# Row-wise weight products on one Trainium2 core: the high and low weight matmuls of each left block, in two passes or in pairs

## The chip, the cores and the metric

One core of a Trainium2 chip runs the whole program in one launch. The metric is the device time of one execution in microseconds (us); the times shown are of three executions of the kernel before.

## The reference, cut to what matters

The program computes two transformer blocks of two layers each on 256 tokens of width 2048, all in float32. Most of its arithmetic is products of the token rows with weights: input projections, output projections and an MLP.

```python
x = first_block(x, ...)                  # 2 layers: h @ w_in, three mixers, y @ w_out
for l in range(DEPTH):                   # 2 layers of the second block
    h = rms_norm_2(x, attn_norm[l])
    proj = h @ w_in[l]
    ...                                  # three attention mixers
    x = x + mixed @ w_o[l]
    h = rms_norm_2(x, mlp_norm[l])
    x = x + jnp.square(jax.nn.relu(h @ w_up[l])) @ w_down[l]
```

## The kernel before, in words

**The products.** TensorE multiplies rounded float32 numbers (fp32r), so each operand is split into a high part (the rounded value) and a low part (what the rounding left). A product is high x high, high x low and low x high, all added up in PSUM. The left operand (the rows, transposed, in `hT_both`, `cT_hi`/`cT_lo` or `uT_hi`/`uT_lo`) is the 128x128 block that stands still in the array; the weights stream past it, 344 to 512 columns in one matmul.

**The weight groups.** The weights come in 988 groups of up to 128 x 1024 numbers, numbered L in the one order in which all products use them. For each group SP issues a load into one of 10 slots of `raw` (line 790); ScalarE copies it, rounded, into one of 4 slots of `w_hi` (line 874, semaphore `hi_ready`); VectorE subtracts that from the raw numbers and leaves the low part in the same bytes, now called `w_lo` (line 1251, semaphore `group_read`); TensorE multiplies by both, and the last matmul counts `group_multiplied`, which frees the slot of `w_hi` and the slot of `raw`. ScalarE and VectorE convert groups two ahead of the one that TensorE is at (`AHEAD = 2`). VectorE also multiplies 192 loads of modulation weights, which use the same slots of `raw` (lines 1407 and 1419), and does much of the mixers' work.

**A row-wise group.** `group_product` (lines 1987 to 2013) does this for all jobs except the up-projections (`high_turned` and `low_turned`, lines 2024 and 2034, where the weights stand still) and two small head-wise products (`heads_product`). A group of 1024 numbers at 512 columns has two chunks c, and there are two token halves t, so four terms (c, t), each with its own left block; the two halves t go to two PSUM banks. Before the change TensorE runs three passes over the four terms: line 2005 multiplies by the high weights, then it waits for `group_read`, line 2008 multiplies the same four left blocks by the low weights, and line 2012 multiplies the low left blocks by the high weights. Where the left operand is still being made (the first groups of a job), the first pass waits for its high part and the last for its low part. The last groups of three jobs are done for one token half at a time (`tail`), so that the first half is ready sooner; there all terms of a pass go to one PSUM bank.

**The order around it.** Each engine has its instructions written in its own fixed order. On TensorE, before the product of group L stand the transposes that prepare left operands (line 1951), and at places listed in tables (`SLIDING_AT`, `LINEAR_AT`, `MLA_AT` and others) the steps of the attention mixers: scores (line 2207), probabilities times values (line 2228), and so on. A matmul that waits therefore holds up every later one, the mixers' too. `busy` (line 2083 before, 2082 after) multiplies the identity by itself a few times while TensorE would idle.

Of the kernel before, what the change touches and what calls it, by code (L numbers as in the profile page):

```python
# [212 lines left out]
def build(nc, io):  # L213
    ctx = ExitStack()
    with ctx:
# [51 lines left out]
        def blocks(ring, slot, cnt, width):  # L267

            return ring[:, slot, 0:cnt * width].rearrange("p (c n) -> p c n", n=width)
        w_hi = sb("w_hi", [P, SPLIT_SLOTS, GROUP], F32R)  # L270

        def hi_blocks(slot, cnt, width):

            pitch = (width + 3) // 4 * 4
            return blocks(w_hi, slot, cnt, pitch)[:, :, 0:width]
# [159 lines left out]
        group_at = []  # L435
# [165 lines left out]
        def pinned(job, i):  # L601

            return job.pinned and i == job.turns

        def bank(job, i, t):

            if job.swept and i == 2 or pinned(job, i):
                return 4 + t
            return 2 * ((job.T + i) % 2) + t
# [1317 lines left out]
        def _(pe):  # L1927
# [26 lines left out]
            def multiply(job, i, j, L, led_to):  # L1954
# [23 lines left out]
                if not job.in_tail(i, j):  # L1978
                    group_product(job, i, j, L, range(TOK), led_to).then_inc(S.group_multiplied, 1)
                    return  # L1980
                mm = group_product(job, i, j, L, (0,), led_to)
                if j == len(job.groups) - 1:
                    mm.then_inc(S.first_token, 1)
                    for back in reversed(range(job.tail)):
                        group_product(job, i, j - back, L - back, (1,)).then_inc(S.group_multiplied, 1)

            def group_product(job, i, j, L, tokens, led_to=None):

                hi, lo = job.lhs
                k0, cnt = job.groups[j]  # L1990
                start, stop = k0 == 0, k0 + cnt == job.chunks
                if pinned(job, i):
                    start, stop = start and job.kind == "ina", stop and job.kind == "ind"
                terms = [(c, t, ps[:, bank(job, i, t), 0:job.width]) for c in range(cnt) for t in tokens]
                wh = hi_blocks(L % SPLIT_SLOTS, cnt, job.width)
                wl = blocks(w_lo, group_at[L] % RAW_SLOTS, cnt, job.width)

                def rows(v, c, t):

                    return v[:, job.lhs0 + k0 + c, t * P:(t + 1) * P]  # L2000
                pe.wait_ge(S.hi_ready, L + 1)
                if led_to:
                    pe.wait_ge(S.lhs_hi, led_to[0])
                for c, t, o in terms:
                    pe.matmul(o, rows(hi, c, t), wh[:, c], start=start and c == 0, stop=False)  # L2005
                pe.wait_ge(S.group_read, group_at[L] + 1)
                for c, t, o in terms:
                    pe.matmul(o, rows(hi, c, t), wl[:, c], start=False, stop=False)  # L2008
                if led_to:
                    pe.wait_ge(S.lhs_ready, led_to[1])  # L2010
                for c, t, o in terms:
                    mm = pe.matmul(o, rows(lo, c, t), wh[:, c], start=False, stop=stop and c == cnt - 1)  # L2012
                return mm
# [377 lines left out]
```

## Time and profile before

| | |
|---|---|
| median of 3 executions | 2918.69 us (2916.41 to 2918.80) |
| span of the profiled execution, first to last instruction | 2916.5 us |
| the profiled execution's own time | not listed apart; its span lies 2.2 us below the median |
| TensorE matmul busy | 2835.1 us, 97% of the span, 14688 matmuls |
| TensorE weight load busy | 2448.1 us, 84%, 14688 loads |
| VectorE busy | 1892.8 us, 65% |
| ScalarE busy | 1442.6 us, 49% |
| mean granted TensorE clock | 0.995 of full |

A matmul's busy time includes its way through the array, so two that follow each other closely overlap in the trace. What a stream of them costs is the distance from one start to the next. A row of the time line with x4 merges four, from the first start to the last end.

### The profile page before, as it was taken

Reading aid. Unit: us, or ns where it says so; the run is one execution under the profiler, and the core shown is the slowest. Engines: PE = TensorE matmul, PEld = TensorE weight load, DVE = VectorE, ACT = ScalarE, POOL = GpSimd, SP = SyncE. Lnnn points to the kernel's source line nnn. Section 1 sums busy time; section 2 is a strip of 40 time slices with the busy share of each in tenths; the row PEclk is TensorE's granted clock in tenths of the full one; section 3 lists DMA queues with packets and bytes.
Section 4 is the critical chain, followed back from the end, with each engine's and each line's share of the span. In section 5 each row is a group of like instructions: output and inputs, shape, how many; then the busy total and the mean of one; then the engine's idle time right before and its main releaser. Section 6 shows DMA issues by size and latency. Waiting matters only on the chain.

```text
span 2916.5 us, 37048 instructions
## 1 busy us (share of the span) xinstructions
PE 2835.1 (97%) x14688; PEld 2448.1 (84%) x14688; DVE 1892.8 (65%) x2395; ACT 1442.6 (49%) x2035; POOL 41.1 (1%) x48
## 2 busy tenths in 40 slices
PE   5998998999999999999999999999999999999998
PEld 5886787898889988888888888899888888888887
DVE  8998998779755566665445554545666654456554
ACT  5445544665546554644334444555546443344443
POOL 0000000000000000000000000000000000000000
PEclk9999999999999999999999999999999999999999
DMA  9996598767655455555665556564445555555653
GB/s 392 366 350 227 188 363 305 257 203 256 241 177 181 146 162 165 176 191 191 194 195 188 188 194 193 176 189 152 160 164 174 190 195 192 194 187 191 207 195 137
DMA packets 173884, 611.89 MB, mean 210 GB/s; under 512 B 19681, under 2 KB 19953, under 8 KB 173073
## 3 DMA queue, kind: packets, MB, share of 16 engines
q1 hardware_dynamic: 170912, 600.42, 60.4%
q0 software_dynamic: 1824, 6.61, 0.8%
q8 instruction: 117, 1.92, 0.3%
q10 hardware_dynamic: 976, 2.51, 0.3%
q14 instruction: 55, 0.44, 0.0%
HBM read 607.34 MB, written 2.11 MB: 209 GB/s over the span
## 4 chain that ended last, share of the span: by engine, by line
PE 86%; DVE 7%; ACT 3%; DMA 2%; issue 1%; SPq 0%; POOL 0%; POOLq 0%; ACTq 0%; DVEq 0%
PE ps L2005 19%; PE ps L2008 19%; PE ps L2012 18%; PE ps L2024 16%; PE ps L2034 8%; PE ps L1951 2%; DVE w_lo L1251 2%; DVE raw L1407 2%; PE ps L2228 1%; DMA raw<-in_w_ina 1%; PE ps L2207 1%; ACT w_hi L874 1%; DMA raw<-in_w_modT 1%; DVE proj L1381 1%; DMA raw<-in_w_in 0%
## 5 line engine op out<-in xcount | busy, mean ns | idle before, releaser
L1251 DVE TENSOR_TENSOR w_lo<-raw,w_hi 128x1024 fp32r<-128x1024 f32 (+4 forms) x988 | 1150.0, 1175 | 865.6 <-ACT w_hi L874 863.0
L874 ACT ACTIVATE w_hi<-raw 128x1024 fp32r<-128x1024 f32 (+4 forms) x988 | 994.6, 1018 | 1174.6 <-PE ps L2012 644.4
L2005 PE MATMUL ps<-w_hi,hT_both 128*128 128x512 f32 (+3 forms) x1824 | 479.3, 384 | 16.4 <-DVE proj L1381 8.4
L2024 PE MATMUL ps<-hT_both,w_hi 128*128 128x512 f32 x2048 | 490.2, 391 | 0.9 <-DVE u L1355 0.9
L2008 PE MATMUL ps<-w_lo,hT_both 128*128 128x512 f32 (+3 forms) x1824 | 463.0, 375 | 0.6 <-DVE w_lo L1251 0.6
L2012 PE MATMUL ps<-w_hi,hT_both 128*128 128x512 f32 (+3 forms) x1824 | 460.1, 374 | 0.0
L2024 PEld LDWEIGHTS ps<-hT_both,w_hi 128*128 128x128 f32 x2048 | 376.1, 188 | 74.1 <-DVE u L1355 1.3
L2008 PEld LDWEIGHTS ps<-w_lo,hT_both 128*128 128x128 f32 x1824 | 340.2, 189 | 51.0 <-DVE w_lo L1251 1.9
L2012 PEld LDWEIGHTS ps<-w_hi,hT_both 128*128 128x128 f32 x1824 | 339.7, 189 | 48.7
L2005 PEld LDWEIGHTS ps<-w_hi,hT_both 128*128 128x128 f32 x1824 | 327.0, 189 | 63.7 <-DVE proj L1381 12.5
L2005 PE MATMUL ps<-w_hi,uT_hi 128*128 128x512 f32 x1024 | 275.1, 390 | 0.0
L2008 PE MATMUL ps<-w_lo,uT_hi 128*128 128x512 f32 x1024 | 274.4, 389 | 0.0
L2012 PE MATMUL ps<-w_hi,uT_lo 128*128 128x512 f32 x1024 | 274.4, 389 | 0.0
L2034 PEld LDWEIGHTS ps<-hT_both,w_lo 128*128 128x128 f32 x2048 | 262.8, 191 | 10.2
L2034 PE MATMUL ps<-hT_both,w_lo 128*128 128x256 f32 x2048 | 265.9, 283 | 0.0
L2008 PEld LDWEIGHTS ps<-w_lo,uT_hi 128*128 128x128 f32 x1024 | 192.2, 188 | 40.1
L2012 PEld LDWEIGHTS ps<-w_hi,uT_lo 128*128 128x128 f32 x1024 | 192.2, 188 | 40.0
L2005 PEld LDWEIGHTS ps<-w_hi,uT_hi 128*128 128x128 f32 x1024 | 191.5, 188 | 39.3
L1407 DVE SCALAR_TENSOR_TENSOR raw<-raw,c_row 128x1024 f32<-128x1024 f32 x176 | 212.7, 1219 | 0.8
L1496 DVE TENSOR_TENSOR hT_both<-hf,hT_both 128x512 fp32r<-128x512 f32 x80 | 55.3, 691 | 54.1 <-ACT hT_both L943 53.5
L1110 ACT ACTIVATE probs<-probs,smax 128x128 f32<-128x128 f32 (+3 forms) x112 | 50.9, 455 | 40.3 <-DVE smax L1576 38.0
L1951 PE MATMUL ps<-cst,proj 128*128 128x128 f32 x292 | 42.2, 276 | 25.2 <-ACT proj L1194 23.8
(255 smaller groups left out, 1563.7 us busy)
## 6 DMA issues: line engine op xcount, KB each, us to landing
raw<-in_w_up SPq DMA_DIRECT2D x256, 512.0 KB, 4.1
raw<-in_w_down SPq DMA_DIRECT2D x256, 512.0 KB, 4.2
raw<-in_w_modT SPq DMA_DIRECT2D x192, 512.0 KB, 5.6
raw<-in_w_rest SPq DMA_DIRECT2D x80, 456.0 KB, 3.4
raw<-in_w_z SPq DMA_DIRECT2D x64, 512.0 KB, 4.4
raw<-in_w_out SPq DMA_DIRECT2D x64, 512.0 KB, 4.4
raw<-in_w_rest SPq DMA_DIRECT2D x48, 344.0 KB, 3.6
raw<-in_w_oa SPq DMA_DIRECT2D x32, 512.0 KB, 3.4
```

The source lines that it names most:

```text
L874: act.activation(hi_blocks(L % SPLIT_SLOTS, c, w), blocks(raw, G % RAW_SLOTS, c, w), ACT.Copy).then_inc(S.hi_ready, 1)
L1110: a = act.activation(e, e, ACT.Exp, bias=smax[:, r, j:j + 1], accum_out=ssum[:, r, j:j + 1])
L1251: dve.tensor_tensor(blocks(w_lo, r, c, w), blocks(raw, r, c, w), hi_blocks(s, c, w).bitcast(F32), ALU.subtract).then_inc(S.group_read, 1)
L1381: dve.tensor_tensor(v, v, ps[:, b:b + TOK, 0:job.width], ALU.add).then_inc(S.dve_evacuated, 1)
L1407: dve.scalar_tensor_tensor(out=w, in0=w, scalar=1.0, in1=c_row[:, part], op0=ALU.mult, op1=ALU.mult, accum_out=mod_part[:, l, block, part: ...
L1496: dve.tensor_tensor(dst_lo[:, 2 * b:2 * b + 2], hf[:, u_ % 2], dst_hi[:, 2 * b:2 * b + 2].bitcast(F32), ALU.subtract).then_inc(S.lhs_ready, 1)
L1951: mm = pe.transpose(ps[0:rows, b, j * P:(j + 1) * P], s, ident)
L2005: pe.matmul(o, rows(hi, c, t), wh[:, c], start=start and c == 0, stop=False)
L2008: pe.matmul(o, rows(hi, c, t), wl[:, c], start=False, stop=False)
L2012: mm = pe.matmul(o, rows(lo, c, t), wh[:, c], start=False, stop=stop and c == cnt - 1)
L2024: pe.matmul(ps[:, bank(job, i, f)], wh[:, c, f * P:(f + 1) * P], hT_both[:, k0 + c].rearrange("p a n -> p (a n)"), start=k0 + c == 0, stop ...
L2034: mm = pe.matmul(ps[:, bank(job, i, f), 0:2 * P], wl[:, c, f * P:(f + 1) * P], hT_hi[:, k0 + c], start=False, stop=k0 + c == job.chunks - 1)
```

## The change

In `group_product` the first two passes become one: for each term (c, t) the matmul by the high weights is followed directly by the matmul of the same left block by the low weights, into the same PSUM bank. The wait for `group_read`, which stood ahead of the second pass, now stands ahead of the first matmul of the group. The third pass stays. Every matmul is still issued, with the same operands. The diff:

```diff
                 pe.wait_ge(S.hi_ready, L + 1)
+                pe.wait_ge(S.group_read, group_at[L] + 1)
                 if led_to:
                     pe.wait_ge(S.lhs_hi, led_to[0])
                 for c, t, o in terms:
                     pe.matmul(o, rows(hi, c, t), wh[:, c], start=start and c == 0, stop=False)
-                pe.wait_ge(S.group_read, group_at[L] + 1)
-                for c, t, o in terms:
                     pe.matmul(o, rows(hi, c, t), wl[:, c], start=False, stop=False)
                 if led_to:
                     pe.wait_ge(S.lhs_ready, led_to[1])
```

TensorE's order at a group of the down-projection in the second block (`uT_hi`, `uT_lo` are the left operand), before:

```order
L2005 MATMUL ps<-w_hi,uT_hi 128x512 [waits hi_ready,u_split]
L2005 MATMUL ps<-w_hi,uT_hi 128x512 x3
L2008 MATMUL ps<-w_lo,uT_hi 128x512 [waits group_read]
L2008 MATMUL ps<-w_lo,uT_hi 128x512 x3
L2012 MATMUL ps<-w_hi,uT_lo 128x512 x4
```

and of the changed kernel, whose lines 2006, 2007 and 2011 are the high, the low and the last product:

```order
L2006 MATMUL ps<-w_hi,uT_hi 128x512 [waits group_read,hi_ready,u_split]
L2007 MATMUL ps<-w_lo,uT_hi 128x512
L2006 MATMUL ps<-w_hi,uT_hi 128x512
L2007 MATMUL ps<-w_lo,uT_hi 128x512
L2006 MATMUL ps<-w_hi,uT_hi 128x512
L2007 MATMUL ps<-w_lo,uT_hi 128x512
L2006 MATMUL ps<-w_hi,uT_hi 128x512
L2007 MATMUL ps<-w_lo,uT_hi 128x512
L2011 MATMUL ps<-w_hi,uT_lo 128x512 x4
```

The two passes of four have become four pairs, and the wait for `group_read` has moved up by four matmuls. The same on TensorE in the last input projection of the first block (`rest`, 344 columns), where the scores of the sliding-window mixer (line 2207, 2206 after) stand behind a group; before:

```order
L2005 MATMUL ps<-w_hi,hT_both 128x344 [waits hi_ready]
L2005 MATMUL ps<-w_hi,hT_both 128x344 x3
L2008 MATMUL ps<-w_lo,hT_both 128x344 [waits group_read]
L2008 MATMUL ps<-w_lo,hT_both 128x344 x3
L2012 MATMUL ps<-w_hi,hT_both 128x344 x4
L2207 MATMUL ps<-k1T,q1T 128x256 [waits dve_bank_drained]
L2207 MATMUL ps<-k1T,q1T 128x256 x3
```

and after:

```order
L2006 MATMUL ps<-w_hi,hT_both 128x344 [waits group_read,hi_ready]
L2007 MATMUL ps<-w_lo,hT_both 128x344
L2006 MATMUL ps<-w_hi,hT_both 128x344
L2007 MATMUL ps<-w_lo,hT_both 128x344
L2006 MATMUL ps<-w_hi,hT_both 128x344
L2007 MATMUL ps<-w_lo,hT_both 128x344
L2006 MATMUL ps<-w_hi,hT_both 128x344
L2007 MATMUL ps<-w_lo,hT_both 128x344
L2011 MATMUL ps<-w_hi,hT_both 128x344 x4
L2206 MATMUL ps<-k1T,q1T 128x256 [waits dve_bank_drained]
L2206 MATMUL ps<-k1T,q1T 128x256 x3
```

The mixer's scores stand where they stood, behind the group's last product. The orders of VectorE, ScalarE, GpSimd and of the DMA queue do not move.

## Rows read from the trace of the kernel before

**Rows 1.** The page, part 1: busy time, share of the span, instructions
```profile
PE 2835.1 (97%) x14688; PEld 2448.1 (84%) x14688; DVE 1892.8 (65%) x2395; ACT 1442.6 (49%) x2035; POOL 41.1 (1%) x48
```
**Rows 2.** Windows: stretch, length, busy us of PE, PEld, DVE, ACT, POOL, clock, DMA, GB/s
```profile
100.00:150.00 50.00, 46.38 (x227) 41.32 (x226) 49.90 (x72) 21.21 (x25) 0.00 (x0) 1.00 0.97 367
...
600.00:700.00 100.00, 99.41 (x608) 91.33 (x607) 82.71 (x143) 59.47 (x95) 1.28 (x1) 1.00 0.70 235
```
**Rows 3.** Groups by line: busy us, mean ns of one, then idle before them, releaser
```profile
L1251 DVE TENSOR_TENSOR w_lo<-raw,w_hi 128x1024 fp32r<-128x1024 f32 x734 | 891.2, 1224 | 708.2 <-ACT w_hi L874 706.8
L874 ACT ACTIVATE w_hi<-raw 128x1024 fp32r<-128x1024 f32 x734 | 768.6, 1057 | 981.7 <-PE ps L2012 540.0 <-PE ps L2034 366.0 <-DMA raw<-in_w_out 37.2
```
**Rows 4.** The page, part 5: the second pass of `group_product` from `hT_both`
```profile
L2008 PE MATMUL ps<-w_lo,hT_both 128*128 128x512 f32 (+3 forms) x1824 | 463.0, 375 | 0.6 <-DVE w_lo L1251 0.6
```
**Rows 5.** Time line, down-projection, first and second tile: start, length (us), engine, line
```profile
1366.52 1.07 PE L2012 MATMUL ps<-w_hi,uT_lo 128*128 128x512 f32 x4
1367.43 1.07 PE L2005 MATMUL ps<-w_hi,uT_hi 128*128 128x512 f32 x4
...
1440.87 1.07 PE L2005 MATMUL ps<-w_hi,uT_hi 128*128 128x512 f32 x4
...
1441.77 1.07 PE L2008 MATMUL ps<-w_lo,uT_hi 128*128 128x512 f32 x4
1442.22 1.23 DVE L1251 TENSOR_TENSOR w_lo<-raw,w_hi 128x1024 fp32r<-128x1024 f32 x1 [1.49 <-ACT w_hi L874]
```
**Rows 6.** Chain of waits, an up-projection (256 columns) and a product of the linear mixer
```profile
359.02 2.69 PE ps L2301 x24
...
1195.34 1.91 PE ps L2034 x16
```
**Rows 7.** Time line: transposes (all blocks different), identity by itself (one block repeated)
```profile
469.04 1.04 PE L1951 MATMUL ps<-cst,proj 128*128 128x128 f32 x8
...
858.26 2.40 PE L2083 MATMUL ps<-cst 128*128 128x128 f32 x20
```
**Rows 8.** One line asked for, L2083: count, duration min/median/max
```profile
L2083 PEld LDWEIGHTS ps<-cst x84: 188/192/338, 31.7 to 862.8; 128*128 128x128 f32 x84
L2083 PE MATMUL ps<-cst x84: 273/275/582, 31.7 to 862.9; 128*128 128x128 f32 x84
```
**Rows 9.** Time line near the end, one token half, all in one PSUM bank
```profile
2898.94 0.62 PE L2005 MATMUL ps<-w_hi,uT_hi 128*128 128x512 f32 x2
2899.39 0.61 PE L2008 MATMUL ps<-w_lo,uT_hi 128*128 128x512 f32 x2
2899.84 0.62 PE L2012 MATMUL ps<-w_hi,uT_lo 128*128 128x512 f32 x2
```
**Rows 10.** Time line of the second group of the program (450 columns)
```profile
39.19 2.10 DVE L1251 TENSOR_TENSOR w_lo<-raw,w_hi 128x900 fp32r<-128x900 f32 x2 [0.15 <-ACT w_hi L874]
...
39.38 0.98 PE L2005 MATMUL ps<-w_hi,hT_both 128*128 128x450 f32 x4
...
40.34 0.70 PEld L2008 LDWEIGHTS ps<-w_lo,hT_both 128*128 128x128 f32 x4 [0.35 <-DVE w_lo L1251]
```
**Rows 11.** Time line in the 344-column projection
```profile
575.00 2.45 DVE L1251 TENSOR_TENSOR w_lo<-raw,w_hi 128x688 fp32r<-128x688 f32 x3 [2.25 <-ACT w_hi L874]
...
575.02 0.90 PE L2005 MATMUL ps<-w_hi,hT_both 128*128 128x344 f32 x4 [0.69 <-ACT w_hi L874]
...
575.93 0.89 PE L2008 MATMUL ps<-w_lo,hT_both 128*128 128x344 f32 x4
...
654.37 2.44 DVE L1251 TENSOR_TENSOR w_lo<-raw,w_hi 128x688 fp32r<-128x688 f32 x3
...
655.30 0.89 PE L2008 MATMUL ps<-w_lo,hT_both 128*128 128x344 f32 x4 [0.59 <-DVE w_lo L1251]
```
**Rows 12.** Time line around a fall of the clock (450 columns)
```profile
197.90 1.46 PE L2005 MATMUL ps<-w_hi,hT_both 128*128 128x450 f32 x4 [2.50 <-DVE proj L1381]
...
202.01 0.98 PE L2005 MATMUL ps<-w_hi,hT_both 128*128 128x450 f32 x4
```

## The prediction, made before the changed kernel ran

> **What bounds the kernel now.** I read the page first: TensorE is busy 97% of the span, VectorE 65%, ScalarE 49% [rows 1]. Matmuls overlap in that account, so next the stretches: from 600 us on TensorE fills over 99 us of nearly every 100 (the first such stretch is shown), while in the first 200 us the DMA engines are filled to 0.97 or more and TensorE has 46 of 50 us [rows 2]. So a load bound holds at the start, TensorE itself for the last 2300 us. Then the groups by line, to see how far the conversions run ahead: the subtraction (line 1251) idles for ScalarE's copy, and the copy idles for TensorE to free a slot [rows 3]. Both wait for their customer, so they are early. The second pass, the one whose wait the change moves, waited 0.6 us for line 1251 in the whole run [rows 4]. Last the time line, for the distance from one matmul to the next.
>
> **The price of one matmul.** In the down-projection two passes of four 512-column matmuls start 0.90 or 0.91 us apart [rows 5], and in the tail two start 0.45 us apart [rows 9]: 0.226 us each, about 0.2267 where more of them are averaged. At 2.4 GHz, which the granted clock of 1.00 is [rows 2], 512 columns take 213.3 ns; 13.4 ns are left over. 16 matmuls of 256 columns take 1.91 us [rows 6], so 119.4 each: 106.7 of columns and 12.7 over. The distance follows the columns. The weight load of each, of which there are as many as matmuls [rows 1], lies beside the matmul ahead of it. Only with 128 columns does it show: transposes start (1.04-0.275)/7 = 0.109 us apart [rows 7, 8], where the columns are 53 ns.
>
> **Part 1, the order of the matmuls.** Nothing is removed or added: 2868 pairs of the lines 2005 and 2008 (1824 from `hT_both`, 1024 from `uT_hi`, 20 from `cT_hi`) and their weight loads are all issued, in another order. Three things differ for a matmul.
>
> (a) The second of a pair has the left block of the first. Whether the repeated load costs less isn't in the trace for these shapes. From below: if no load were needed and everything above the columns went with it, 13.4 ns would be saved in each second matmul, 2868 x 0.0134 = 38 us. From above: the identity multiplied by itself, the same block again and again, starts (2.40-0.275)/19 = 0.112 us apart, against 0.109 of transposes with a new block each [rows 7]; 3 ns more in each would be 2868 x 0.003 = 9 us lost. Those 84 matmuls have 84 loads of the full 188 ns [rows 8]: repetition saves no load. And ordinary mixer products with changing blocks also take 2.69/24 = 0.112 [rows 6], so the 3 ns belong to the form and not to the repetition. I take 0 for (a), by rows 7 and 8, the only ones with a repeated block.
>
> The Trainium skill ("TensorE: Matmul & The Clock Gate", Back-to-back issue gap) gives N / 2.4 + 2.5 ns for matmuls that follow each other, 215.8 ns at 512 columns. The trace's 226.7 doesn't agree. If the 10.9 ns between them were the new weights' and fell away in every second matmul of a pair, the rule would give an estimate of 31 us saved; by the rows it is none.
>
> (b) Both matmuls of a pair add into one PSUM bank, at the same addresses; before, the two token halves took turns. The tail of the last job already does this: with one token half all matmuls of its passes, and across the passes, go to one bank, and they start 0.226 us apart as everywhere else [rows 5, 9]. 0.
>
> (c) The stream changes between `w_hi` and `w_lo` at each matmul. Across the change of pass it did so before, and 1440.87 to 1441.77 holds such a change at no extra [rows 5]. 0.
>
> **Part 2, the wait that moves up.** `group_read` must now be there before the first matmul, four matmuls earlier (0.91 us at 512 columns, 0.81 at 450, 0.62 at 344). I paired the k-th subtraction of line 1251 with the first matmul of the k-th group, for the 720 groups of `group_product`. In the down-projections the subtraction ends 5.6 us before its group begins in the typical case: one that starts at 1442.22 and takes 1.23 [rows 5] is for the group that TensorE reaches at about 1449.0, two groups of 12 x 0.2267 = 2.72 us after 1443.6. There the wait is always met. In 12 groups it isn't.
> - Second group of the program: the first of the two subtractions ends at 40.28, its low pass began at 40.34 [rows 10]. Now the first pass begins there, and the end moves by that pass, 0.81 us. The groups at 71.86 (subtraction over at 72.86), 116.07 (116.73) and 159.32 (159.97), read from the time line in the same way, give 0.81, 0.63 and 0.62; four small ones (36.8 to 66.6 us) 0.06 + 0.16 + 0.08 + 0.03. Together 3.2 us before 160 us.
> - The 344-column groups at 575.02 and 653.92: their low passes began 0.06 us after the subtraction ended, at 575.93 and 655.30 [rows 11]. Each moves by 0.62.
> - Three more at 694.65, 1038.61 and 2061.51, where the first pass began about 0.1 us before the subtraction's end: 0.19 + 0.15 + 0.15. Together 1.7 us after 570 us.
>
> The first 3.2 us fall in the stretch that loads bound: TensorE has about 3.6 us of slack in every 50 there [rows 2], a group late by 0.8 us makes it up before 200 us, and the loads it releases have others in flight before them. I cost them at 0; if that cover is gone, they cost their 3.2. The last 1.7 us fall where TensorE has no slack, so they reach the end. What is queued behind the waiting matmul is the group's other eleven and then, at 575 us, the scores of the sliding-window mixer, which come 0.62 us later; VectorE, which waits for scores, had idled 2.25 us before its subtractions there [rows 11] and can take that. The release of the slot is at the group's end as before, and moves by no more.
>
> **Part 3, several waits on one matmul.** The first matmul of a group now carries two or three waits (`hi_ready`, `group_read`, `u_split`). In the down-projection's first tile it had two before, and there the last pass of one group (1366.52) and the first of the next (1367.43) are 0.91 us apart, no more than within a group [rows 5]. I take 0; three on one matmul I can bound only by that, 0 again.
>
> Sum: 2916.5 + 0 + 1.7 = 2918.2 for the profiled execution's span; its own time isn't listed, the median of the three is 2.2 us above the span, so 2918.7 + 1.7 = 2920.4 us for the median. That is 0.06%; a difference under about 0.2% (5.8 us) can't be told from none for this kernel, whose three executions spread over 2.4 us.
>
> **The rivals.**
> 1. *The repeated left block makes the second matmul cheaper.* For it: a distance 13 ns above the columns' time in every matmul, so there is something to win, and loads busy 84% of the span [rows 1]. Against: the identity's loads are all there and start no closer [rows 7, 8]; the distance follows the columns, so the load isn't what TensorE waits for [rows 5, 6]. Price: up to 38 us, 2920.4 - 38 = 2882; at half, 2901. It decides from 2.6 ns a pair on, (5.8+1.7)/2868. Chance 0.09. A small saving of ScalarE's or VectorE's by other timing adds 0.01 on this side.
> 2. *The early wait spreads, slower.* Place: the first 200 us and the mixers of the second layer, 570 to 700 us. The 3.2 us of the start are not absorbed, since each late release delays a load in the stretch where loads bound, and TensorE's longer pauses let its clock fall. At 197.90, after 2.50 us of idling, three passes took until 202.01, 4.11 us for 12 matmuls that take 12 x 0.2035 = 2.44 at full clock [rows 12]: 1.7 us a fall. Two more falls and the 3.2: 2920.4 + 3.2 + 3.4 = 2927.0. It decides when more than 5.8 us of waits reach the end. Against: all direct delays together are 4.9 us, and the pauses at 575 and 654 us, 0.69 and 0.59 us now [rows 11], come to 0.69 + 0.91 = 1.6 and 655.30 - 654.07 = 1.2 us (the pass before ends at 654.07), less than the 2.50 after which the clock fell. Chance 0.11. The skill's same page (A second HAM failure mode) says that short pauses between groups of matmuls can make the clock swing; by that this rival would come true, and the pause at 575 us in this trace, with the clock at full, doesn't show it.
> 3. *Pairs in one bank or with one block cost some ns.* The upper bound of (a), 9 us: 2929. Against: rows 9. Chance 0.03.
>
> **How the numbers follow.** Forecast 0.76, rivals 0.10, 0.11, 0.03. The forecast's own range is 2916.4 (the fastest of before) to 2918.7 + 4.9 = 2923.6. With 0.24 outside it, one rival has to be taken in, and the slower one lies nearer: to 2928. At the low end I allow 1 ns a pair, 3 us, from 2918.7 + 0 down: 2915. Faster by over 0.2%: 0.10; within: 0.76; slower: 0.14.
>
> **What the profile would show.** Right: the merged rows of the lines 2006 and 2007 alternate, 0.227 us apart; 14688 loads and matmuls as now; line 2006 waits for line 1251 at about 40, 72, 116, 159, 575 and 654 us, 3 to 5 us in all; the group of eight still takes 8 x 0.227 = 1.81 us. Wrong in (a): starts at 0.213 to 0.22 us at every second matmul, or fewer loads than 14688. Wrong in (b): starts alternating 0.227 and more. Wrong in part 2: a sum of waits of line 2006 on line 1251 above 6 us, or more falls of the clock than the first 500 us have now.

## The result and the profile after

Five executions each, in the same rounds: before 2916.41 us in the median, after 2925.58 us (2924.67 to 2929.75), a ratio of 1.0030 with a 95% interval of 1.0019 to 1.0042. That is 9.2 us slower, inside the range of the prediction, but beyond its forecast of 1.7 us. A second comparison of 11 executions with 33 of before (below, `after_again`) gave 1.0019 (1.0010 to 1.0028), 6.1 us. The two medians put the loss at 0.2 to 0.3%; the intervals reach from 0.1 to 0.4%.

The 33 executions of before in the second comparison spread over 9.5 us (2913.2 to 2922.7), and most of that goes with the time that TensorE's clock was at its lower level. The mean clock of each execution is recorded to three places: the 12 at 0.994 had a mean span of 2917.6 us, the 12 at 0.995 one of 2915.7, the 8 at 0.996 one of 2912.7. So a single trace can't show a loss of a few us by its span; places have to be compared. The profiled execution of after (2929.75 us, span 2927.8) was the slowest of its five.

The page of after, part 1 and two groups of part 5:

```profile
PE 2840.2 (97%) x14688; PEld 2451.9 (84%) x14688; DVE 1893.7 (65%) x2395; ACT 1442.4 (49%) x2035; POOL 41.0 (1%) x48
...
L1251 DVE TENSOR_TENSOR w_lo<-raw,w_hi 128x1024 fp32r<-128x1024 f32 (+4 forms) x988 | 1149.9, 1175 | 871.9 <-ACT w_hi L874 868.6
...
L2007 PE MATMUL ps<-w_lo,hT_both 128*128 128x512 f32 (+3 forms) x1824 | 685.3, 376 | 0.0
```

All 14688 weight loads are still there, no fewer than in [rows 1]. The mean length of the low-weight matmul is 376 ns, 375 in [rows 4]. Its group's busy time has gone from 463 to 685 us without any more work: the four of a pass used to overlap each other, and now each overlaps its neighbours of the other line.

The distance from one matmul to the next, in the time line of after in a down-projection, and in the tail, where everything goes to one bank:

```profile
1452.20 0.39 PE L2006 MATMUL ps<-w_hi,uT_hi 128*128 128x512 f32 x1
1452.42 0.39 PE L2007 MATMUL ps<-w_lo,uT_hi 128*128 128x512 f32 x1
1452.65 0.39 PE L2006 MATMUL ps<-w_hi,uT_hi 128*128 128x512 f32 x1
1452.88 0.39 PE L2007 MATMUL ps<-w_lo,uT_hi 128*128 128x512 f32 x1
...
1453.56 1.07 PE L2011 MATMUL ps<-w_hi,uT_lo 128*128 128x512 f32 x4
1454.46 0.39 PE L2006 MATMUL ps<-w_hi,uT_hi 128*128 128x512 f32 x1
...
2910.51 0.39 PE L2007 MATMUL ps<-w_lo,uT_hi 128*128 128x512 f32 x1
2910.74 0.39 PE L2006 MATMUL ps<-w_hi,uT_hi 128*128 128x512 f32 x1
```

High to low, 0.22 to 0.23 us; low to high, 0.23; a pass of four 0.90; across a group's start, which now carries three waits, no more. It is what [rows 5, 9] show of before. From the group at 1149.35 us of before to the one at 1814.84, 665.49 us, after takes 665.49 us too.

Who waited for the subtraction, in the answer on line 1251 of after:

```profile
  ACT w_hi L874: 868.6, 629
who waited for it (us, times):
  PE ps L2006: 5.5, 8
```

8 waits, 5.5 us, against 0.6 us in [rows 4]. Two of them, at the 344-column projection:

```profile
583.88 2.45 DVE L1251 TENSOR_TENSOR w_lo<-raw,w_hi 128x688 fp32r<-128x688 f32 x3 [2.25 <-ACT w_hi L874]
...
584.90 0.39 PE L2006 MATMUL ps<-w_hi,hT_both 128*128 128x344 f32 x1 [1.71 <-DVE w_lo L1251]
...
663.99 2.44 DVE L1251 TENSOR_TENSOR w_lo<-raw,w_hi 128x688 fp32r<-128x688 f32 x3
...
665.00 0.40 PE L2006 MATMUL ps<-w_hi,hT_both 128*128 128x344 f32 x1 [1.32 <-DVE w_lo L1251]
```

They are the groups of [rows 11]: the subtraction starts as late as before, relative to its surroundings, and TensorE stands 1.71 and 1.32 us where it stood 0.69 and 0.59. A ninth wait, 0.79 us at the second group, is put down to ScalarE's copy (below); with it the sum is 6.3 us, just over the 6 us that the prediction had named as a sign against part 2. Aligned by group, the trace of after is 2.5 us late at 200 us, 8.9 at the start of the 344-column projection, 10.6 after it, and 10.9 from there to 2000 us.

In the stretch between, the start of the second layer, the clock of this trace fell twice more than in before. The windows, and the pause ahead of the second fall:

```profile
500.00:510.00 10.00, 7.76 (x27) 5.89 (x27) 9.36 (x13) 4.61 (x6) 0.00 (x0) 0.83 0.83 326
520.00:530.00 10.00, 6.80 (x28) 5.18 (x28) 7.01 (x10) 3.73 (x6) 0.00 (x0) 0.90 0.99 350
```

```profile
527.52 0.47 PE L2006 MATMUL ps<-w_hi,hT_both 128*128 128x512 f32 x1 [3.20 <-ACT hT_both L943]
...
529.02 0.63 PE L2006 MATMUL ps<-w_hi,hT_both 128*128 128x512 f32 x1
529.44 0.63 PE L2007 MATMUL ps<-w_lo,hT_both 128*128 128x512 f32 x1
```

After 3.20 us of idling the matmuls come to be 0.42 to 0.43 us apart, which is 512 columns at 1.2 GHz. More falls than before were another sign that the prediction had named. Whether these falls belong to the change was the first thing to find out.

### The profile page after: what moved, and what is told of

The parts are those of the page before. It is cut to its first block, busy times and chain, and to the rows that moved or that the text cites. A ratio compares the mean times of both kernels' runs of the same rounds, so it can differ in the third digit from the quotient of the medians.

```text
span 2927.8 us, 37578 instructions
## 1 busy us (share of the span) xinstructions
PE 2840.2 (97%) x14688; PEld 2451.9 (84%) x14688; DVE 1893.7 (65%) x2395; ACT 1442.4 (49%) x2035; POOL 41.0 (1%) x48
## 4 chain that ended last, share of the span: by engine, by line
PE 86%; DVE 6%; DMA 3%; ACT 3%; issue 1%; SPq 0%; POOL 0%; POOLq 0%; ACTq 0%; DVEq 0%
PE ps L2006 19%; PE ps L2007 19%; PE ps L2011 18%; PE ps L2023 16%; PE ps L2033 8%; PE ps L1951 2%; DVE w_lo L1251 2%; DVE raw L1407 2%; PE ps L2227 1%; DMA raw<-in_w_ina 1%; PE ps L2206 1%; ACT w_hi L874 1%; DMA raw<-in_w_modT 1%; DMA raw<-in_w_in 1%; DVE proj L1381 0%
## 5 line engine op out<-in xcount | busy, mean ns | idle before, releaser
L2006 PE MATMUL ps<-w_hi,hT_both 128*128 128x512 f32 (+3 forms) x1824 | 702.3, 385 | 21.5 <-ACT hT_both L943 7.6
L2007 PE MATMUL ps<-w_lo,hT_both 128*128 128x512 f32 (+3 forms) x1824 | 685.3, 376 | 0.0
L2011 PE MATMUL ps<-w_hi,hT_both 128*128 128x512 f32 (+3 forms) x1824 | 459.0, 373 | 0.0
L2006 PEld LDWEIGHTS ps<-w_hi,hT_both 128*128 128x128 f32 x1824 | 346.1, 190 | 76.5 <-issue 12.0
L2006 PE MATMUL ps<-w_hi,uT_hi 128*128 128x512 f32 x1024 | 399.0, 390 | 0.0
L2007 PE MATMUL ps<-w_lo,uT_hi 128*128 128x512 f32 x1024 | 398.5, 389 | 0.0
L2007 PEld LDWEIGHTS ps<-w_lo,hT_both 128*128 128x128 f32 x1824 | 346.5, 190 | 44.2
L2011 PEld LDWEIGHTS ps<-w_hi,hT_both 128*128 128x128 f32 x1824 | 339.3, 188 | 48.7
```

## The experiments

Theory A: the moved wait is the whole loss, and the pairs are free. Theory B: a pair costs some ns. In the tables of a result "before" is the kernel before in the same rounds on the same chip.

### The wait alone, and the pairs by place

`wait_up` keeps the three passes and moves the wait:

```diff
                 if led_to:
                     pe.wait_ge(S.lhs_hi, led_to[0])
+                pe.wait_ge(S.group_read, group_at[L] + 1)
...
-                pe.wait_ge(S.group_read, group_at[L] + 1)
```

> The three passes as before, only the wait for group_read stands ahead of the first pass. Theory A (the moved wait is all of the loss, the pairs cost nothing): as slow as the change, about +9 us (+6 to +12), with more falls of the clock than before between 200 and 540 us. Theory B (the pairing itself costs, 9 us over 2868 pairs, 3 ns each): within 3 us of before.

`pairs_second` and `pairs_first` choose by group between the body of the change and that of before:

```diff
+                if L >= jobs["c20"].L:
+                    pe.wait_ge(S.group_read, group_at[L] + 1)
+                    for c, t, o in terms:
+                        pe.matmul(o, rows(hi, c, t), wh[:, c], start=start and c == 0, stop=False)
+                        pe.matmul(o, rows(hi, c, t), wl[:, c], start=False, stop=False)
+                else:
...
```

> Pairs and the early wait in the second block only (from c20 on, 863 us into the trace of before), passes in the first. Theory A: +0.3 us (two waits of 0.15), not to be told from before. Theory B: 3 ns for each of the pairs there, about 2150 of 2868, +6.5 us.

> Pairs and the early wait in the first block only. Theory A: all of the loss, about +9 us, all of it before 700 us. Theory B: about 700 of the 2868 pairs, +2 us.

> The change once more, on the chip and in the rounds of the other three: +7 to +12 us against before. The number of falls of the clock in its profile tells whether the two more (at 504 and 528 us) belong to every execution; theory A says the waits come again at the same places, and the falls may not.

| kernel | median us, 11 executions | ratio to before (2917.88 us, 33) | 95% interval |
|---|---|---|---|
| wait_up | 2922.40 | 1.0014 | 1.0005 to 1.0023 |
| pairs_second | 2917.49 | 1.0003 | 0.9995 to 1.0012 |
| pairs_first | 2924.10 | 1.0021 | 1.0012 to 1.0029 |
| after_again | 2924.02 | 1.0019 | 1.0010 to 1.0028 |

The counts of pairs in these expectations were off: 1056 lie in the first block and 1812 in the second, so theory B wanted 3.2 and 5.4 us. It falls all the same: the 1812 cost at most 3.5 us by the interval, and the wait alone, without a pair, costs 4.5 us. The 665.49 us above say the same. But 4.5 us is under the 6 to 12 us expected of `wait_up`, and the 6.1 us of `after_again` under its 7 to 12: A is right on where the loss comes from, and these expectations, taken from the first comparison, were too large.

The falls of the clock are not the mechanism. Before the last 10 us, the traces of before, `pairs_second` and `pairs_first` hold 27 us at the lower clock each, `after_again` 31, and `wait_up`, slower than before in the median, 17. In the mean over the executions the clock is 0.99455 for `after_again` and 0.99482 for before, a difference worth about 0.8 us of the 6. At the same recorded clock of 0.994 the mean spans are 2923.1 us (8 executions) and 2917.6 us (12). The two falls at 504 and 528 us made this one trace long.

### Where the first block loses

`pairs_start` has the pairs in the first 64 groups, `pairs_middle` in the groups from 64 to the end of the first block (which is 263, not 271; the diff as above, with `L < jobs["z0"].L` and `jobs["z0"].L <= L < jobs["c20"].L`).

> Pairs and the early wait only in the first 64 groups (the four quarters of the first input projection, up to 209 us). If the load-bound stretch absorbs late groups, as the prediction had it: within 1 us of before. If it does not: +3.2 us from the direct waits there, up to +5 us with what follows from them.

> Pairs and the early wait only in groups 64 to 271 (209 to 863 us of before). By the waits at 575, 654 and 695 us: +1.4 us (predicted) to +1.7 us (what all four profiles with the early wait show between the groups 152 and 209); more than +3 us if the stretch of the second layer's first projection (470 to 540 us) loses time of its own there.

`pairs_start` took 2922.82 us, before 2918.28 (27 executions): 1.0017 (1.0008 to 1.0026), 4.5 us. `pairs_middle` 2919.34: 1.0005 (0.9996 to 1.0014), 1.1 us. So most of the loss comes from the stretch that the prediction had absorbing it. How a delay leaves TensorE can be seen at one load. The DMA queue at 40 us, before and after:

```profile
39.58 0.33 SPq L790 DMA_DIRECT2D raw<-in_w_modT  x1
42.27 0.33 SPq L790 DMA_DIRECT2D raw<-in_w_ina  x1
```

```profile
40.11 0.33 SPq L790 DMA_DIRECT2D raw<-in_w_modT  x1
43.60 0.33 SPq L790 DMA_DIRECT2D raw<-in_w_ina  x1
```

and between the two in the trace of after:

```profile
39.67 2.10 DVE L1251 TENSOR_TENSOR w_lo<-raw,w_hi 128x900 fp32r<-128x900 f32 x2 [0.15 <-ACT w_hi L874]
...
40.87 0.44 PE L2006 MATMUL ps<-w_hi,hT_both 128*128 128x450 f32 x1 [0.79 <-ACT w_hi L874]
...
42.59 0.98 PE L2011 MATMUL ps<-w_hi,hT_both 128*128 128x450 f32 x4
```

The second group of the program waits for its subtraction (its idle time is put down to ScalarE, which came a little before), its last pass ends 0.7 us later, counted from the first group's start, and the load that needs its slot is issued 3.49 us after the one ahead of it instead of 2.69. SP issues in order, so every later load is behind it: counted in the same way, the loads stay 0.7 us late up to 60 us.

The gap of those two loads sorts eleven traces without exception (all but `left_test`, which keeps the old wait too and has 2.44): 2.48 to 2.72 us in before and the four kernels with the old wait in this group, 3.18 to 3.49 in the six with the early one. The time from the first group to group 60 (37 to 198 us of before) does so too: 161.1 to 162.3, mean 161.7, in the five; 163.0 to 163.9, mean 163.6, in the six. The start loses 1.8 us of the 3.2 of direct waits.

Which waits these are shows in VectorE's own instructions, the same one taken in each trace and timed from the first group. Up to the one at 65.5 us of before the six take 0.50 us more in the mean (29.86 against 29.36), but there the two sets overlap, 28.7 to 30.1 in the five and 29.4 to 30.6 in the six: kernels with the old wait lose time at this place as well. From there to 174.6 us the difference is 0.07 us. The waits at 72 and 116 us fall in this stretch: they make TensorE and the loads 0.8 us late, and both have caught up within 30 us, before VectorE needs what is late. From 174.6 to 192.3 us the six take 18.0 to 19.3, the five 17.1 to 17.8 us, in the mean 1.27 us more. This is the wait at 159 us: the load behind its group is issued 2.80 to 2.85 us after the one ahead in the six, 2.02 to 2.05 in the five, and the loads are still 0.8 us later at 184 us, where VectorE waits for copies and these for loads. In before:

```profile
179.68 1.10 DVE L1251 TENSOR_TENSOR w_lo<-raw,w_hi 128x900 fp32r<-128x900 f32 x1 [0.72 <-ACT w_hi L874]
...
181.29 0.96 ACT L874 ACTIVATE w_hi<-raw 128x900 fp32r<-128x900 f32 x1 [1.64 <-DMA raw<-in_w_ind]
...
182.28 1.09 DVE L1251 TENSOR_TENSOR w_lo<-raw,w_hi 128x900 fp32r<-128x900 f32 x1 [0.36 <-ACT w_hi L874]
```

and in `after_again`:

```profile
179.99 1.22 DVE L1407 SCALAR_TENSOR_TENSOR raw<-raw,c_row 128x1024 f32<-128x1024 f32 x1 [0.75 <-DMA raw<-in_w_modT]
...
182.10 1.10 DVE L1251 TENSOR_TENSOR w_lo<-raw,w_hi 128x900 fp32r<-128x900 f32 x1 [0.88 <-ACT w_hi L874]
...
184.36 0.96 ACT L874 ACTIVATE w_hi<-raw 128x900 fp32r<-128x900 f32 x1 [2.29 <-DMA raw<-in_w_ind]
...
185.35 1.09 DVE L1251 TENSOR_TENSOR w_lo<-raw,w_hi 128x900 fp32r<-128x900 f32 x1 [1.01 <-ACT w_hi L874]
```

No kernel has the early wait at one of these groups alone, so this split of the 1.8 us rests on the traces.

### The 13 late groups, and all the others

The last pair of kernels splits by the table that the prediction was made from: the groups whose low weights came after, or within 0.03 us of, the group's start.

```diff
+                if L not in (0, 1, 10, 11, 12, 14, 30, 46, 165, 195, 209, 327, 689):
...
```

is `pairs_but_late`; `pairs_late_only` has `in` in place of `not in`.

> Pairs and the early wait in 707 of the 720 groups; the 13 whose low weights came later than (or within 0.03 us of) the group's start in the trace of before (0, 1, 10, 11, 12, 14, 30, 46, 165, 195, 209, 327, 689) keep the passes. If the loss comes from these waits alone: within 1.5 us of before, the second group's load release at its old place, and the distance from group 152 to 209 as before. If the pairing or the early wait elsewhere costs: +3 to +6 us remain.

> The complement: pairs and the early wait in those 13 groups only. If the waits alone make the loss: +4 to +6.5 us, as the whole change, with +1.7 us between groups 152 and 209. If not: +2 us or less.

| kernel | median us | ratio to before (2918.28 us, 20) | 95% interval |
|---|---|---|---|
| pairs_but_late (707 groups) | 2920.03, 11 executions | 1.0006 | 0.9997 to 1.0014 |
| pairs_late_only (13 groups) | 2923.23, 10 executions | 1.0020 | 1.0011 to 1.0030 |

13 groups of 720 make most of the loss, 4.9 us in the median; the interval of the other 707 holds no change, and up to 4 us more. In the trace, the first matmul of group 152 and of group 209, in `pairs_late_only` and then in `pairs_but_late`:

```profile
545.16 0.32 PE L2011 MATMUL ps<-w_hi,hT_both 128*128 128x344 f32 x1
...
695.64 0.47 PE L2007 MATMUL ps<-w_hi,hT_both 128*128 128x512 f32 x1
```

```profile
547.03 0.32 PE L2007 MATMUL ps<-w_hi,hT_both 128*128 128x344 f32 x1
...
695.85 0.39 PE L2011 MATMUL ps<-w_hi,hT_both 128*128 128x512 f32 x1
```

150.48 and 148.82 us. This stretch is the steadiest ruler of the case: 148.82 to 148.85 in before and the three other kernels with the old wait there, 150.47 to 150.52 in the six with the early one, whatever happened earlier in the execution. (Group 209 itself then takes 0.10 us more in the six.) Its loss is 1.67 us, in the stretch where TensorE is the bound and nothing absorbs it.

### The wait later instead of earlier

`low_last` turns the change round: where the left operand is ready, the low weights come last, a pass later than before.

```diff
                 for c, t, o in terms:
                     pe.matmul(o, rows(hi, c, t), wh[:, c], start=start and c == 0, stop=False)
+                if not led_to:
+                    for c, t, o in terms:
+                        pe.matmul(o, rows(lo, c, t), wh[:, c], start=False, stop=False)
                 pe.wait_ge(S.group_read, group_at[L] + 1)
...
```

> The other way: in groups whose left operand is ready the low weights come last, two passes behind the high ones, in three passes. TensorE's waits for line 1251 at 575 and 654 us (about 0.3 and 0.6 to 0.8 us in before) fall away: the distance from group 152 to group 209 shortens by about 1.0 us, the whole by 1 to 1.5 us, which the timing may not tell from before. If waits for the low weights cost nothing in the end: no change.

2918.28 us, ratio 0.9997 (0.9988 to 1.0006): not to be told from before. In its trace the stretch from group 152 to 209 is 148.22 us, 0.63 less than in before and 2.3 less than in after, where 1.0 was expected. The direction is that of the waits; it is no version that can be called faster.

### The price of a repeated left block

> Before the second block, in place of 10 multiplications of the identity, 4 x 32 rounded-float32 matmuls: 128 columns with one left block, 128 columns with two in turn, then the same two with 512 columns. If a repeated left block is loaded again at full price: starts 0.109 us apart in both 128-column rows and 0.227 in both 512-column rows. If the chip spares the repeated load: 0.067 or less against 0.109 with 128 columns. If a repeated block costs more: over 0.109 and 0.227. The whole gets up to 20 us longer.

```diff
-                    busy(10)
+                    for width in (P, 4 * P):
+                        for lefts in (1, 2):
+                            for k in range(32):
+                                pe.matmul(ps[:, 4, 0:width], hT_hi[:, k % lefts, 0:P],
+                                          hT_both[:, 2].rearrange("p a n -> p (a n)")[:, 0:width], start=True, stop=True)
```

The one execution took 2937.03 us, 18.8 more than before in the median, where up to 20 were expected. The time line of its four parts, asked for in four windows: 128 columns with one left block, with two in turn, then 512 columns with one and with two:

```profile
858.28 3.69 PE L2099 MATMUL ps<-hT_both 128*128 128x128 f32 x32
...
861.80 3.62 PE L2099 MATMUL ps<-hT_both 128*128 128x128 f32 x31
...
865.67 7.01 PE L2099 MATMUL ps<-hT_both 128*128 128x512 f32 x30
...
872.74 6.96 PE L2099 MATMUL ps<-hT_both 128*128 128x512 f32 x30
```

With 128 columns, (3.69-0.275)/31 = 0.110 us against (3.62-0.275)/30 = 0.112 for changing blocks; with 512, (7.01-0.389)/29 = 0.228 against 0.227. The 0.110 holds one distance of 0.058 us, the first; the 30 behind it are 0.112 in the mean, as with two blocks. The line has 128 loads for its 128 matmuls, of 187 to 192 ns each. So a repeated block is loaded again, and costs what changing blocks cost. At 128 columns, where matmuls start twice as far apart as the columns' 53 ns, a saving had the most room to show.

## Why the prediction was right, and where it was not

**The price of one matmul, and part 1.** Right in all three. (a) The repeated left block: taken at 0 between -38 and +9 us; measured 0, by 14688 loads, by the unchanged 0.227 us, by `left_test` and by `pairs_second`. The Trainium skill's rule of N / 2.4 + 2.5 ns ("TensorE: Matmul & The Clock Gate", Back-to-back issue gap), which that section gives for a matmul by itself and not for a stream with its weight loads, disagrees with these rows as it did with those of before. The prediction's estimate of 31 us was the 11 ns between the two; they don't go when the block is repeated. (b) One bank: 0, as the tail of before had shown; the pairs of a down-projection start 0.227 us apart. (c) 0.

**Part 2, the sizes of the waits.** Right in place. 8 waits were recorded, 5.5 us in all (6.3 with the second group's), where 3 to 5 us were announced; `pairs_late_only` shows that the 13 groups found by pairing subtractions with groups in the trace of before are the ones that matter. (The prediction says 12, but its list has 13.) The later waits were priced at 1.7 us together: 1.43 for the three of groups 165, 195 and 209, which measured 1.67 and 0.10 more within 209, and 0.30 for the two in the second block. Those measured 0.8: from group 240 to group 960 the five traces with the early wait at both take 2040.0 to 2040.1 us, the six without it 2039.1 to 2039.6, in the mean 2039.2.

**The step that failed is "I cost them at 0"**, of the first 3.2 us. Its ground was that TensorE has 3.6 us of slack in every 50 and that released loads "have others in flight before them", so that a group late by 0.8 us makes it up before 200 us. For the waits at 72 and 116 us that is what the traces show. It failed in the mean at the second group, and in every trace at the wait at 159 us. There TensorE's slack is not what counts: its end of a group releases a slot, SP waits for that slot in order, and VectorE waits for what lands in it. The traces show 1.8 us of the 3.2 lost by 200 us, some 0.5 of it by 66 us and 1.3 after 174 us; the timing of `pairs_start` says 4.5. The note "if that cover is gone, they cost their 3.2" was the nearer value. [rows 2] warned of it with VectorE's 49.9 of 50 us, but didn't tell which waits would come through: the one at 116 us falls in just that stretch and was made up.

**The rivals.** The faster one and the one of some ns a pair are refuted. The slower one, that the early wait spreads, is what happened in its first half (late releases), and was given 0.11. Its second half, more falls of the clock, is in the first trace; the others hold 17 to 31 us at the lower clock against 27. The mean clocks don't go one way: against before, `after_again` is lower by 0.0003, `pairs_start` by 0.0007 (an estimate of 1.4 us by the slope below), `wait_up` higher by 0.0005.

**Part 3**, several waits on one matmul: 0. With three waits that are met, the first matmul of a group starts 0.227 us after the one ahead of it, as within a group.

**What stays open.** The traces account for 1.8 + 1.7 + 0.8 = 4.3 us. The timing says 9.2 in the first comparison, 6.1 in the second (2.9 to 8.2), 4.9 for the 13 groups alone. Some 2 us may come from 200 to 545 us. There single traces differ by more than that from one execution to the next, with the clock's falls and the loads at the start of the second layer: from group 60 to group 152 the six traces with the early wait at the start take 341.8 to 354.3 us, mean 347.8, the five others 346.1 to 347.9, mean 347.2. No run here isolates it.

Part of the scatter is the clock's. Along the executions of before the time falls by 2.1 to 2.5 us for each 0.001 of mean clock. With this taken out, an estimate with a standard error of 0.4 to 0.6 us, `after_again` is 5.5 us slower than before, `wait_up` 6.1, `pairs_first` 5.9, `pairs_second` 1.4, `pairs_start` 3.0, `pairs_middle` 2.5, `pairs_late_only` 4.9, `pairs_but_late` 0.7, and `low_last` 0.9 faster. (If the early wait itself changes the clock's falls, this takes out a part of the effect.) By it the 13 groups are nearly the whole change. The true size lies close to the 0.2% that was to part "within" from "slower", and "slower" had been given 0.14.

## What to carry to other kernels

A wait that is moved earlier costs what the trace of before shows group by group: pair each producer with its consumer and list the few that are late, rather than the mean or the total. Then ask of each late one not only whether the engine that waits has slack, but whose work its end releases, and whether that engine is going to wait for just these deliveries: here the same 0.8 us was made up after 72 and 116 us and lost after 159 us, and only the traces told them apart. Putting matmuls of the same left block next to each other is worth nothing here while each matmul brings its own load, and the load lies beside the stream.

## What the runs showed of the hardware that had not been expected

A rounded-float32 matmul pays for its weight load in full even when the same block is already in the array: at 128 columns 32 matmuls start 0.112 us apart with one block as with two (the first distance left out), each with a load of 187 to 192 ns.

The time at the lower clock varies between executions of one program: the mean clock of the 33 executions of before ran from 0.993 to 0.996 and the span with it, from 2920.9 us (one execution at 0.993) to a mean of 2912.7. A straight line through clock and time takes up 79% of the variance of these 33 executions, and 42% and 81% in the 27 and the 20 of the other comparisons.
